# Two experts' token rows selected transposed, chunk by chunk between their products

## The chip, the cores and the metric

The kernel runs on one core of a Trainium2 chip. The metric is the device time of one execution in microseconds; the median of three runs is given with their lowest and highest. A profile of one further execution gives the rows. Times in rows are microseconds from the start of the profiled span.

## What is computed

One decoder layer on 256 tokens of 2048 channels, float32: a mixer (dilated window attention beside retention), a LayerNorm, and then a mixture of 32 experts. Each token picks one of four expert groups and in it the two best of eight experts. The part that matters here:

```python
def expert_block(args):
    xb, e = args
    hid = jax.nn.silu(xb @ w_gate[e]) * (xb @ w_up[e])
    return hid @ w_down[e]
```

w_gate[e] and w_up[e] are 2048 x 512, w_down[e] is 512 x 2048; xb are the rows of the tokens that chose expert e. The second LayerNorm follows.

## The kernel before

The first 1140 us are the mixer, the router and the first LayerNorm. Then come 32 experts, called items, each with 32 places for token rows (ROWS = 32; an expert with more tokens gets more items at the end). The weights are read from memory once each, 12.6 MB an expert, into four buffers W0 to W3 of 4 MB by DMAs that SyncE's queue issues in program order. Kind 0 is the first half of gate and up (channels in j = 0), kind 1 the second half, kind 2 the down matrix. A load waits until the products that read the buffer before have been counted: gu_used is raised by 2 after each half of gate and up, d_used after halves of the down product. Expert 1's second half comes in parts: pairs of 512 KB that wait for gu_part, which item 0's products raise behind chunks k = 1, 3 and 5 of the first half, and a last one that waits for gu_used. Expert 0's second half has its own buffers WT0. These orders are written out by hand, and the change leaves SyncE's order as it is.

For each item the token rows are made in four steps. z is the normalised layer output (tile Z, also named ZN), tokens on the partitions.
- VectorE writes a selection matrix SEL, 128 tokens x 32 places for each of the two token tiles, 1 where the token goes to that place. For item 0 and 1 this comes straight from the members and their ranks (SEL and SEL1); for later items select_next counts the places in YD down by 32 and compares again.
- `gather` on TensorE: SEL is the stationary operand, z streams through, eight products in four column groups of 32 columns each. The result has 4 x 32 rows in PSUM.
- `rows_copy` on ScalarE copies it to XG, `turn_rows` on TensorE transposes it in four blocks of 128 x 128.
- `rows_scaled` on ScalarE scales the 16 channel chunks with LayerNorm's scale and bias into XE, one instruction each. XE is the stationary operand of `gate_up`.

`gate_up(item, ..., q, ...)` multiplies chunk k of XE (32 columns) with gate and up (512 columns each). Even k use column groups 0 and 1, odd k groups 2 and 3, so four products run side by side. Item 0 sums in bank 6, item 1 in bank 0. Each product is two records in the profile. `hidden` on VectorE and `hidden_tanh` on ScalarE make the hidden values, `turn_hidden` transposes them (HB to HT), `down` multiplies with the down matrix, `spread_rows` adds the rows back to the tokens.

Around the first two items TensorE's order before is: gather(0), place_rows, turn_rows(0), count_rows, gate_up(0) first half with gather(1) behind its chunk 3 and turn_rows(1) behind chunk 5, gate_up(1) first half, gate_up(0) second half, gather(2), gate_up(1) second half, turn_hidden(0). place_rows and count_rows are three full-width products each that VectorE needs for the places of the later items.

Of the kernel before, what the change touches and what calls it, by code (L numbers as in the profile page):

```python
# [37 lines left out]
P = 128  # L38
# [3 lines left out]
KD = D // P  # L42
# [227 lines left out]
def build(nc, x, positions, w_in, w_branch_attn, w_branch_ret, w_out, ln1_scale, ln1_bias,  # L270
# [92 lines left out]
    XG0 = at("XG0", 176, [QC])  # L363
    XG1 = at("XG1", 178, [QC])
    W11 = at("W11", 44, [2 * HID])
    SEL1 = at("SEL1", 201.25, [TOK, ROWS])
# [146 lines left out]
    members, ranked, xe_first = sem("members"), sem("ranked"), sem("xe_first")  # L513
# [92 lines left out]
    def xe_bank(item):  # L606

        return SPREAD + 1 if isinstance(item, int) and item == 1 else XE_BANK

    def xg(item):  # L610

        return (XG0, XG1)[item] if isinstance(item, int) and item < 2 else XG

# [227 lines left out]
    def _(pe):  # L841
# [276 lines left out]
        def gather(item):  # L1118

            pe.wait_ge(sel_ready, item * TOK + TOK)  # L1120
            if isinstance(item, int) and item < 2:
                pe.wait_ge(z_norm, TOK)
            else:
                pe.wait_ge(xe_stored, item * QS)
            sel, bank = (SEL1 if isinstance(item, int) and item == 1 else SEL), xe_bank(item)
            for t in range(TOK):
                channels = ZN[:, t].rearrange("p (j c h k) -> p j h c k", j=QS, h=QD // QS, k=KQ * QS // QD)
                for m in range(QD):
                    mm = pe.matmul(PS[m * ROWS:(m + 1) * ROWS, bank].rearrange("p (c k) -> p c k", c=P),  # L1129
                                   sel[:, t], channels[:, m // 2, m % 2], start=t == 0, stop=t == TOK - 1)  # L1130
            mm.then_inc(gathered, 1)

        def turn_rows(item):

            pe.wait_ge(xg_stored, item + 1)
            for k in range(KD // QD):
                mm = pe.transpose(PS[:, xe_bank(item), k * P:(k + 1) * P],  # L1137
                                  xg(item)[:].rearrange("p (c k) -> p k c", c=P)[:, k], rid)
            mm.then_inc(xe_turned, 1)

        def gate_up(item, k4, q, rows, more=False, gathered_between=None, last=False):

            by_place = isinstance(item, int) and item < 2 and q == 0
# [6 lines left out]
            for m in range(2):  # L1150
# [10 lines left out]
            for j in range(KQ):  # L1161
                k = KQ * q + j
                odd = j % 2
                if by_place and j < KQ - 1:
                    pe.wait_ge(xe_first, item * (KQ - 1) + j + 1)
                elif by_place:
                    pe.wait_ge(xe_stored, item * QS + 1)
# [11 lines left out]
                if gathered_between is not None and j % 2 and j < KQ - 1:  # L1179
                    mm.then_inc(gu_part, 1)  # L1180
                    if j == 3:
                        gather(gathered_between)
                    elif j == 5:
                        turn_rows(gathered_between)
            mm.then_inc(gu_used, 2)
# [278 lines left out]
    def _(act):  # L1464
# [179 lines left out]
        def rows_copy(item):  # L1644
            act.wait_ge(gathered, item + 1)
            act.activation(xg(item)[:], PS[:, xe_bank(item)], ACT.Copy).then_inc(xg_stored, 1)

        def rows_scaled(item, buf):

            first = isinstance(item, int) and item < 2  # L1650
            act.wait_ge(xe_turned, item + 1)
            for j in range(QS):
                for k in range(KQ):
                    if first and j == 0 and k:
                        last.then_inc(xe_first, 1)
                    at_k = KQ * j + k
                    c0 = at_k % 4 * P + at_k // 4 * ROWS
                    last = act.activation(XE[:, buf, at_k], PS[:, xe_bank(item), c0:c0 + ROWS], ACT.Identity,  # L1658
# [22 lines left out]

        rows_copy(0)
        rows_scaled(0, 0)
        rows_copy(1)
        rows_scaled(1, 1)
# [777 lines left out]
```

## Time and profile before

| | |
|---|---|
| median of three runs | 2062.95 us (2062.85 to 2064.05) |
| profiled execution, its own time | 2060.22 us |
| span of its rows | 2058.1 us |
| TensorE matmul busy | 1766.7 us, 86% of the span |
| VectorE busy | 994.9 us, 48% |
| ScalarE busy | 757.1 us, 37% |
| mean DMA rate over the span | 299 GB/s |
| scaling of one chunk on ScalarE (L1658), 512 of them | median 0.41 us |
| copy to XG on ScalarE (L1646), 32 of them | median 0.60 us |
| share of DMA W<-in_w_expert_up_dram in the chain that ended last | 21% |
| share of DMA W<-in_w_expert_down_dram in it | 11% |

The span is what lies between the first and the last instruction that was profiled; the execution's own time is 2.1 us longer. Busy time of TensorE is a sum of modelled durations that overlap. The granted clock is a share of 2.4 GHz; 0.50 is 1.2 GHz.

### The profile page before, as it was taken

What the parts mean: (1) busy time and instruction counts of PE and PEld (TensorE: products, weight loads), DVE (VectorE), ACT (ScalarE), POOL (GpSimd) and SP (SyncE); (2) the same over time, 40 slices, a digit from 0 to 9 for tenths busy, and PEclk for the clock granted to TensorE, in tenths of its full rate; (3) what the DMA queues carried; (4) which work ended last, traced back from release to release, by engine and by line L of the source; (5) the groups of instructions that cost most, each with busy time, mean ns of one, the idle gap of its engine ahead of it and who ended that gap; (6) DMA issues with size and microseconds to landing.
All of it is one profiled execution on the core that took longest, in us unless ns stands there. A gap on an engine that the chain in (4) does not pass through costs nothing.

```text
span 2058.1 us, 25311 instructions
## 1 busy us (share of the span) xinstructions
PE 1766.7 (86%) x9868; PEld 1141.9 (55%) x9868; DVE 994.9 (48%) x1469; ACT 757.1 (37%) x1321; POOL 15.3 (1%) x34
## 2 busy tenths in 40 slices
PE   9999999999999999999999986666566666666667
PEld 7888888888888888888888541111112111111222
DVE  5454454555444444566565564334433433343357
ACT  5444444344444444354443422222222222222221
POOL 0000000000000000000000000000000000000000
PEclk9999999999999999999999988887888888887888
DMA  7556655455556555467677999999999999999998
GB/s 247 194 175 189 199 175 176 150 184 187 191 181 194 172 185 178 155 188 238 218 279 287 381 428 425 429 431 429 427 430 433 430 426 429 431 430 427 430 428 367
DMA packets 139042, 615.07 MB, mean 299 GB/s; under 512 B 14228, under 2 KB 14900, under 8 KB 117840
## 3 DMA queue, kind: packets, MB, share of 16 engines
q1 hardware_dynamic: 138240, 611.75, 77.5%
q0 software_dynamic: 720, 2.18, 0.6%
q8 instruction: 58, 0.95, 0.2%
q14 instruction: 24, 0.20, 0.0%
HBM read 609.61 MB, written 2.36 MB: 297 GB/s over the span
## 4 chain that ended last, share of the span: by engine, by line
PE 54%; DMA 33%; issue 10%; DVE 2%; ACT 0%; SPq 0%; DVEq 0%; POOL 0%; POOLq 0%
DMA W<-in_w_expert_up_dram 21%; PE PS L593 14%; PE PS L595 14%; PE PS L594 14%; DMA W<-in_w_expert_down_dram 11%; PE PS L1173 5%; PE PS L1224 2%; PE PS L962 1%; PE PS L1314 0%; PE PS L1129 0%; DVE ZACC L2234 0%; PE PS L1052 0%; DMA VC<-VS 0%; PE PS L1295 0%; PE PS L939 0%
## 5 line engine op out<-in xcount | busy, mean ns | idle before, releaser
L570 DVE TENSOR_TENSOR WL<-RAW,WH 128x1024 fp32r<-128x1024 f32 x384 | 457.4, 1221 | 403.9 <-ACT WH L566 402.5
L566 ACT ACTIVATE WH<-RAW 128x1024 fp32r<-128x1024 f32 x384 | 394.5, 1058 | 261.6 <-PE PS L595 199.8
L593 PE MATMUL PS<-WH,XH 128*128 128x512 f32 x1216 | 480.0, 395 | 0.1
L595 PE MATMUL PS<-WH,XL 128*128 128x512 f32 x1216 | 474.0, 390 | 0.0
L594 PE MATMUL PS<-WL,XH 128*128 128x512 f32 x1216 | 473.3, 389 | 0.0
L1173 PE MATMUL PS<-W,XE 128*32 128x512 f32 x2016 | 277.3, 698 | 135.0 <-DMA W<-in_w_expert_up_dram 133.6
L2234 DVE TENSOR_TENSOR ZACC<-PS,ZACC 128x1024 f32<-128x1024 f32 x124 | 146.0, 1219 | 294.3 <-PE PS L1295 294.3
L1224 PE MATMUL PS<-W,HT 128*32 128x512 f32 x992 | 171.0, 851 | 135.7 <-DMA W<-in_w_expert_down_dram 135.7
L593 PEld LDWEIGHTS PS<-WH,XH 128*128 128x128 f32 x1216 | 228.3, 188 | 49.3 <-issue 1.7
L595 PEld LDWEIGHTS PS<-WH,XL 128*128 128x128 f32 x1216 | 228.2, 188 | 48.3
L594 PEld LDWEIGHTS PS<-WL,XH 128*128 128x128 f32 x1216 | 228.6, 188 | 45.8
L1173 PEld LDWEIGHTS PS<-W,XE 128*32 128x32 f32 x2016 | 70.9, 125 | 322.0 <-issue 187.3
L1224 PEld LDWEIGHTS PS<-W,HT 128*32 128x32 f32 x992 | 38.5, 149 | 242.5 <-DMA W<-in_w_expert_down_dram 124.5
L1658 ACT ACTIVATE XE<-PS,LSB 128x32 f32<-128x32 f32 x512 | 141.1, 414 | 2.6 <-PE PS L1137 1.8
L1664 ACT ACTIVATE HT<-PS 128x128 f32<-128x128 f32 x32 | 9.0, 280 | 222.6 <-PE PS L1192 222.6
L2185 DVE TENSOR_TENSOR GSUM_H<-PS,GB 32x512 f32<-32x512 f32 x31 | 21.0, 679 | 140.2 <-ACT UB L1638 140.2
L1672 ACT ACTIVATE YH<-PS,WROW 128x512 fp32r<-128x512 f32 x29 | 20.0, 690 | 141.2 <-PE PS L1295 119.1
L1637 ACT ACTIVATE GB<-PS 32x512 f32<-32x512 f32 x31 | 18.3, 589 | 142.4 <-PE PS L1173 142.4
L1129 PE MATMUL PS<-Z,SEL 128*32 128x512 f32 x512 | 61.7, 598 | 0.7 <-DVE SEL L2062 0.7
L593 PE MATMUL PS<-WH,RH 128*128 128x512 f32 x128 | 50.2, 392 | 0.0
L595 PE MATMUL PS<-WH,RL 128*128 128x512 f32 x128 | 49.9, 390 | 0.0
L594 PE MATMUL PS<-WL,RH 128*128 128x512 f32 x128 | 49.8, 389 | 0.0
(333 smaller groups left out, 1472.7 us busy)
## 6 DMA issues: line engine op xcount, KB each, us to landing
RAW<-in_w_in_dram SPq DMA_DIRECT2D x304, 512.0 KB, 4.5
W<-in_w_expert_gate_dram SPq DMA_DIRECT2D x61, 2048.0 KB, 28.6
W<-in_w_expert_up_dram SPq DMA_DIRECT2D x61, 2048.0 KB, 33.0
W<-in_w_expert_down_dram SPq DMA_DIRECT2D x28, 4096.0 KB, 35.2
RAW<-in_w_branch_ret_dram SPq DMA_DIRECT2D x32, 512.0 KB, 5.2
RAW<-in_w_out_dram SPq DMA_DIRECT2D x32, 512.0 KB, 6.0
W<-in_w_expert_down_dram SPq DMA_DIRECT2D x7, 2048.0 KB, 30.4
RAW<-in_w_branch_attn_dram SPq DMA_DIRECT2D x16, 512.0 KB, 5.3
```

What stands on the lines that cost most here:

```text
L566: act.activation(WH[:, i % RING], RAW[:, i % RING], ACT.Copy).then_inc(hi_done, 1)
L570: dve.tensor_tensor(WL[:, i % RING], RAW[:, i % RING], WH[:, i % RING].bitcast(F32), ALU.subtract).then_inc(lo_done, 1)
L593: pe.matmul(PS[:, bank + t], hs, wh, start=first and j == 0, stop=False)
L594: pe.matmul(PS[:, bank + t], hs, wl, start=False, stop=False)
L595: mm = pe.matmul(PS[:, bank + t], ls, wh, start=False, stop=end)
L962: mm = pe.transpose(PS[:, bank, h * P:(h + 1) * P], NAT[:, t, h * DH:(h + 1) * DH], ident)
L1129: mm = pe.matmul(PS[m * ROWS:(m + 1) * ROWS, bank].rearrange("p (c k) -> p c k", c=P), sel[:, t], channels[:, m // 2, m % 2], start=t == 0 ...
L1173: mm = pe.matmul(PS[c0:c0 + ROWS, gu_bank(item)], rows[:, k, 0:ROWS], w[:, at_j * HID:(at_j + 1) * HID], start=k < 2, stop=k >= KD - 2)
L1224: mm = pe.matmul(PS[m * ROWS:(m + 1) * ROWS, Y_BANK], HT[:, b], W[pair_q][:, b // KB2, col:col + QC], start=b == 0, stop=b == KH - 1)
L1658: last = act.activation(XE[:, buf, at_k], PS[:, xe_bank(item), c0:c0 + ROWS], ACT.Identity, bias=LSB[:, 1, at_k:at_k + 1], scale=LSB[:, 0, ...
L2185: dve.tensor_tensor(GSUM_H[0:ROWS], PS[0:ROWS, gu_bank(item)], GB[0:ROWS], ALU.add)
L2234: dve.tensor_tensor(z, PS[:, SPREAD + 2 * n:SPREAD + 2 * n + 2], z, ALU.add).then_inc(added, 1)
```

## The change

The rows of items 0 and 1 are no longer gathered and then transposed. A chunk of 128 channels of z, which are columns at a stride of 8 floats, is now the stationary operand, 128 x 128, and the selection matrices of both items side by side (SEL01, 64 columns) stream through it. The result is the transposed chunk of both items at once: 16 such selections of two products each (one for each token tile). ScalarE scales both items' 64 columns in one instruction, 16 instead of 32. There is no rows_copy and no transpose for these items. gather, rows_copy and turn_rows stay for item 2 and later.

TensorE's order becomes a loop over k = 0 to 15: item 0's chunk k, then the selection of chunk k + 2, then, for k below 8, item 1's chunk k. Two selections and place_rows stand ahead of the loop, count_rows behind item 0's chunk 1. The results of the selections alternate between two PSUM banks. The first selection waits for both items' selection matrices. VectorE's select_next(2) overwrites SEL01 and waits for the last of the 16 selections.

```diff
@@ TensorE
+        def gather_turned(k):
+
+            bank, c0 = first_place(k)
+            a = k // KQ * KQ * P + k % KQ
+            for t in range(TOK):
+                mm = pe.matmul(PS[:, bank, c0:c0 + 2 * ROWS], ZN[:, t, a:a + KQ * P - k % KQ:KQ],
+                               SEL01[:, t].rearrange("p i r -> p (i r)"), start=t == 0, stop=t == TOK - 1)
+            mm.then_inc(first_turned, 1)
+
...
-        gather(0)
+        pe.wait_ge(sel_ready, 2 * TOK)
+        pe.wait_ge(z_norm, TOK)
+        gather_turned(0)
+        gather_turned(1)
         place_rows()
-        turn_rows(0)
-        count_rows()
-        pe.wait_ge(sel_ready, 2 * TOK)
-        gate_up(0, 0, 0, take(0), gathered_between=1)
-        gate_up(1, 1, 0, take(1))
-        gate_up(0, 0, 1, take(0))
+        for k in range(KD):
+            q, j = divmod(k, KQ)
+            gate_up(0, 0, q, take(0), places=range(j, j + 1))
+            if k == 1:
+                count_rows()
+            if k + 2 < KD:
+                gather_turned(k + 2)
+            if q == 0:
+                gate_up(1, 1, 0, take(1), places=range(j, j + 1))
         gather(2)
@@ ScalarE
-        rows_copy(0)
-        rows_scaled(0, 0)
-        rows_copy(1)
-        rows_scaled(1, 1)
+        for k in range(KD):
+            act.wait_ge(first_turned, k + 1)
+            bank, c0 = first_place(k)
+            act.activation(XE[:, :, k], PS[:, bank, c0:c0 + 2 * ROWS].rearrange("p (i r) -> p i r", i=2), ACT.Identity,
+                           bias=LSB[:, 1, k:k + 1], scale=LSB[:, 0, k:k + 1]).then_inc(
+                *((xe_first, 1) if k < KD - 1 else (xe_stored, 2 * QS)))
@@ VectorE
         def select_next(item):
 
             dve.drain()
-            dve.wait_ge(gathered, item)
+            if isinstance(item, int) and item == 2:
+                dve.wait_ge(first_turned, KD)
+            else:
+                dve.wait_ge(gathered, item - 2)
```

TensorE's instructions before, from the end of count_rows on: L1116 is its last product, L1173 is gate_up, L1129 gather(1), L1137 turn_rows(1), W_107 item 0's and W_106 item 1's weights.

```order
L1116 MATMUL PS<-AC,RC 128x32
L1173 MATMUL PS<-W_107,XE 32x512 x8
L1129 MATMUL PS<-Z,SEL_129 32x512 x8
L1173 MATMUL PS<-W_107,XE 32x512 x4
L1137 MATMUL PS<-RC,XG_127 128x128 x4
L1173 MATMUL PS<-W_107,XE 32x512 x4
L1173 MATMUL PS<-W_106,XE 32x512 x16
```

The same place now: L1128 is gather_turned with its 64 columns, L1172 gate_up, L1104 the last product of place_rows, L1108 to L1110 count_rows.

```order
L1104 MATMUL PS<-CUM,RC 128x64
L1172 MATMUL PS<-W_107,XE 32x512 x2
L1128 MATMUL PS<-SEL_127,Z 128x64 x2
L1172 MATMUL PS<-W_106,XE 32x512 x2
L1172 MATMUL PS<-W_107,XE 32x512 x2
L1108 MATMUL PS<-CUM,RC 128x32
L1109 MATMUL PS<-AC,RC 128x32
L1110 MATMUL PS<-AC,RC 128x32
L1128 MATMUL PS<-SEL_127,Z 128x64 x2
L1172 MATMUL PS<-W_106,XE 32x512 x2
L1172 MATMUL PS<-W_107,XE 32x512 x2
L1128 MATMUL PS<-SEL_127,Z 128x64 x2
```

The runs of 8, 4, 4 and 16 products in column groups have become pairs, and a full-width pair stands behind every two pairs.

VectorE's instructions at select_next(2), before, with the semaphores they wait for: YD are the places counted down, SEL the selection matrix for item 2, G and V what the router's weights are made from.

```order
L2075 TENSOR_REDUCE YPOS<-PICK 128x4
L2147 TENSOR_SCALAR YD<-YPOS 128x4
L2094 TENSOR_SCALAR YD<-YD 128x4 [waits gathered]
L2084 TENSOR_SCALAR SELF<-RC,YD 128x32 x2
L2087 SCALAR_TENSOR_TENSOR SEL<-RC,YD,SELF 128x32 x2
```

And now:

```order
L2076 TENSOR_REDUCE YPOS<-PICK 128x4
L2151 TENSOR_SCALAR YD<-YPOS 128x4
L2098 TENSOR_SCALAR YD<-YD 128x4 [waits first_turned]
L2085 TENSOR_SCALAR SELF<-RC,YD 128x32 x2
L2088 SCALAR_TENSOR_TENSOR SEL<-RC,YD,SELF 128x32 x2
```

The instructions are the same; the wait in their middle is now for the 16th selection instead of gather(1).

## Rows read from the trace of the kernel before

**Rows 1.** Busy time by stretch: stretch, length, engines, PEclk, DMA share, GB/s.
```profile
1154.00:1162.00 8.00, 8.00 (x74) 3.49 (x70) 6.32 (x39) 7.07 (x27) 0.00 (x0) 1.00 0.97 350
...
1300.00:1900.00 600.00, 384.89 (x2760) 111.76 (x2760) 238.30 (x390) 161.38 (x459) 0.00 (x0) 0.83 1.00 429
```

**Rows 2.** Chain that ended last, in order of time: start, us, what.
```profile
1224.78 21.30 DMA W<-in_w_expert_down_dram
...
1956.17 32.99 DMA W<-in_w_expert_up_dram
```

**Rows 3.** Timeline of SyncE's queue: start us, us, issue of a DMA.
```profile
1154.16 0.35 SPq L764 DMA_DIRECT2D W<-in_w_expert_gate_dram  x1
...
1163.09 0.43 SPq L655 DMA_DIRECT2D W<-in_w_expert_up_dram  x1
1171.31 0.33 SPq L673 DMA_DIRECT2D W<-in_w_expert_down_dram  x1
1177.85 0.33 SPq L655 DMA_DIRECT2D W<-in_w_expert_gate_dram  x1
...
1192.77 0.38 SPq L655 DMA_DIRECT2D W<-in_w_expert_up_dram  x1
1218.37 0.33 SPq L655 DMA_DIRECT2D W<-in_w_expert_gate_dram  x1
```

**Rows 4.** DMA issues at 1154.16, 1163.09, 1171.31, 1192.77: KB, us to landing.
```profile
W<-in_w_expert_gate_dram SPq DMA_DIRECT2D x1, 512.0 KB, 4.4
...
W<-in_w_expert_up_dram SPq DMA_DIRECT2D x1, 2048.0 KB, 13.6
...
W<-in_w_expert_down_dram SPq DMA_DIRECT2D x1, 4096.0 KB, 15.6
...
W<-in_w_expert_up_dram SPq DMA_DIRECT2D x1, 2048.0 KB, 33.4
```

**Rows 5.** Timeline of VectorE and TensorE, 1148 to 1172 us: start, us, instruction.
```profile
1148.80 0.42 DVE L2066 SCALAR_TENSOR_TENSOR SEL<-RC,PS,AC 128x32 f32<-128x32 f32 x2
1148.94 1.92 PE L1129 MATMUL PS<-Z,SEL 128*32 128x512 f32 x16 [0.70 <-DVE SEL L2062]
...
1150.80 0.43 PE L1108 MATMUL PS<-AC,RC 128*128 128x64 f32 x2
...
1151.26 0.41 PE L1110 MATMUL PS<-CUM,RC 128*128 128x64 f32 x2
...
1152.53 0.39 PE L1116 MATMUL PS<-AC,RC 128*128 128x32 f32 x2
...
1152.89 2.09 PE L1173 MATMUL PS<-W,XE 128*32 128x512 f32 x16
...
1165.91 1.90 PE L1129 MATMUL PS<-Z,SEL 128*32 128x512 f32 x16
1167.63 3.62 PE L1173 MATMUL PS<-W,XE 128*32 128x512 f32 x32
1171.18 0.66 PE L1192 MATMUL PS<-RC,HB 32*128 32x32 f32 x4
```

**Rows 6.** Timeline of VectorE at select_next(2) and hidden(0).
```profile
1159.24 0.17 DVE L2094 TENSOR_SCALAR YD<-YD 128x4 f32<-128x4 f32 x1
...
1159.95 0.41 DVE L2087 SCALAR_TENSOR_TENSOR SEL<-RC,YD,SELF 128x32 f32<-128x32 f32 x2
...
1167.38 0.68 DVE L2185 TENSOR_TENSOR GSUM_H<-PS,GB 32x512 f32<-32x512 f32 x1 [3.08 <-ACT UB L1638]
```

**Rows 7.** Weight loads by line, ns min/median/max: L1137 stride 4, L1052 contiguous.
```profile
L1137 PEld LDWEIGHTS PS<-RC,XG x128: 195/212/220, 1151.6 to 2003.0; 128*128 128x128 f32 x128
...
L1052 PEld LDWEIGHTS PS<-WR,ZT x16: 192/192/203, 1141.5 to 1143.2; 128*128 128x128 f32 x16
```

**Rows 8.** A stretch at the lower clock, and gate_up in it.
```profile
1210.00:1215.00 5.00, 4.23 (x24) 1.30 (x28) 3.51 (x5) 0.00 (x0) 0.00 (x0) 0.50 0.99 419
...
1211.93 6.20 PE L1173 MATMUL PS<-W,XE 128*32 128x512 f32 x32
```

More of the change, by code:

```diff
@@ L604, in gu_bank, with first_place @@
         return 6 if isinstance(item, int) and item == 0 else GU_BANK
[L606 to L612, printed above, removed]
+    def first_place(k):
+        return (XE_BANK, SPREAD + 1)[k % 2], k // 2 * 2 * ROWS
     def norm_bank(j):
@@ L1120, in gather @@
             pe.wait_ge(sel_ready, item * TOK + TOK)
[L1121 to L1125, printed above, removed]
+            pe.wait_ge(xe_stored, item * QS)
             for t in range(TOK):
@@ L1128, in gather, with gate_up @@
                 for m in range(QD):
-                    mm = pe.matmul(PS[m * ROWS:(m + 1) * ROWS, bank].rearrange("p (c k) -> p c k", c=P),
-                                   sel[:, t], channels[:, m // 2, m % 2], start=t == 0, stop=t == TOK - 1)
+                    mm = pe.matmul(PS[m * ROWS:(m + 1) * ROWS, XE_BANK].rearrange("p (c k) -> p c k", c=P),
+                                   SEL[:, t], channels[:, m // 2, m % 2], start=t == 0, stop=t == TOK - 1)
             mm.then_inc(gathered, 1)
+        def gather_turned(k):
[5 more added lines that the diff above has]
+            mm.then_inc(first_turned, 1)
         def turn_rows(item):
-            pe.wait_ge(xg_stored, item + 1)
+            pe.wait_ge(xg_stored, item - 1)
             for k in range(KD // QD):
-                mm = pe.transpose(PS[:, xe_bank(item), k * P:(k + 1) * P],
-                                  xg(item)[:].rearrange("p (c k) -> p k c", c=P)[:, k], rid)
+                mm = pe.transpose(PS[:, XE_BANK, k * P:(k + 1) * P],
+                                  XG[:].rearrange("p (c k) -> p k c", c=P)[:, k], rid)
             mm.then_inc(xe_turned, 1)
-        def gate_up(item, k4, q, rows, more=False, gathered_between=None, last=False):
-            by_place = isinstance(item, int) and item < 2 and q == 0
+        def gate_up(item, k4, q, rows, more=False, last=False, places=range(KQ)):
+            by_place = isinstance(item, int) and item < 2
             if not by_place:
@@ L1149, in gate_up @@
                 pe.wait_ge(part_landed, 16 * 6)
-            for m in range(2):
+            for m in range(2) if places[0] == 0 else ():
                 if apart:
@@ L1160, in gate_up @@
                     pe.wait_ge(w_landed[pair_q][1], item * 8 + (16 * loads_until(q, k4, (0, 1)) - 8 * k4))
-            for j in range(KQ):
+            for j in places:
                 k = KQ * q + j
                 odd = j % 2
-                if by_place and j < KQ - 1:
-                    pe.wait_ge(xe_first, item * (KQ - 1) + j + 1)
+                if by_place and k < KD - 1:
+                    pe.wait_ge(xe_first, k + 1)
                 elif by_place:
-                    pe.wait_ge(xe_stored, item * QS + 1)
+                    pe.wait_ge(xe_stored, 2 * QS)
                 for m in range(2):
@@ L1178, in gate_up @@
                         pe.wait_ge(late_landed[m], 16)
-                if gathered_between is not None and j % 2 and j < KQ - 1:
+                if isinstance(item, int) and item == 0 and q == 0 and odd and j < KQ - 1:
                     mm.then_inc(gu_part, 1)
[L1181 to L1185, printed above, removed]
+            if places[-1] == KQ - 1:
+                mm.then_inc(gu_used, 2)
         def turn_hidden(item):
@@ L2061, in _ @@
         for t in range(TOK):
[L2062 removed]
+            dve.scalar_tensor_tensor(SEL01[:, t, 0], RC[:, R_IOTA:R_IOTA + ROWS], PS[:, 6, 2 * t:2 * t + 1],
                                      AC[:, t, 0:1].broadcast_to((P, ROWS)), ALU.is_equal,
```

20 lines of the change are left out of this document (7 added, 13 removed).

## The prediction

> **What bounds the kernel now.** I read the stretches first, then the chain that ended last, then the DMA issues with their landings, and last the timeline of the stretch that the change touches. In [rows 1] the reader is to see a DMA share of 1.00 at 429 GB/s from 1300 to 1900 us, and 350 GB/s in the 8 us from 1154 to 1162, at nearly the same share. The chain in order of time is made of loads of expert weights from 1224 us on [rows 2]: TensorE waits for them and not they for it, down to 1989 us. So from here on the time of the end is the time at which the stream of weights gets through its fixed bytes, and the question is not what the first two experts cost on TensorE, but whether the queue of loads runs dry sooner or later than now. All gains are bounded by what the stream loses now between 1154 and 1162 us: 8 x (429 - 350) / 429 = 1.5 us.
>
> **How a load lands.** From the issues [rows 3] and their times to landing [rows 4] a rule can be read off. The 512 KB load issued at 1154.16 landed after 4.4 us; its bytes at 429 GB/s are 1.2 us, so 3.2 us are delay. A load thus lands at the later of (landing of the one before, its issue + 3.2), plus its bytes at 429 GB/s (2048 KB 4.9 us, 4096 KB 9.8 us). Test: the up half issued at 1163.09 landed at 1176.7; the whole down matrix issued at 1171.31 should land at 1176.7 + 9.8 = 1186.5, and landed at 1171.31 + 15.6 = 1186.9. Its slack was 1176.7 - 3.2 - 1171.31 = 2.2 us: an issue later by more than that leaves the queue empty, and nothing gives that back. The next thin place is the load issued at 1218.37: the one before it (1192.77 + 33.4) landed at 1226.2, so its slack was 4.6 us. The loads between have more: at 1177.85 it is 1186.9 - 3.2 - 1177.85 = 5.9, and it grows from there to 1192.77, whose load took 33.4 us to land.
>
> **What is removed.** On TensorE two gathers and two sets of four transposes; on ScalarE two copies of 0.6 us (table above) and 16 of 32 scalings. ScalarE's part of that is worth nothing: the rows of TensorE follow each other from 1152.89 on without an idle time in front that names ScalarE [rows 5]. TensorE's part is 2 x 1.7 us for the gathers and the transposes beside them, and it comes back below as full-width products.
>
> **What is added: the order on TensorE.** Instead of runs of 16 products in four column groups, each channel chunk k is now: two products of expert 0 in two column groups, two full-width selections (128x128 stationary, 64 columns), two products of expert 1 in the same two groups; from k = 8 expert 0 alone. Expert 1's products for k and expert 0's for k + 1 use opposite groups and stand next to each other, so they run together. Price of one round, from [rows 5]:
> - A product of 512 columns is two records in one column group. gather(2)'s 16 records run from 1165.91 to the start of the next line at 1167.63, 1.72 us for four steps of four records, 0.43 us a step. With two or four groups at work a round needs two steps, 0.86 us; behind k = 8 half the array stands idle in it.
> - From column groups to full width: the last of the gather's four steps starts at 1148.94 + 3 x 0.43 = 1150.23, and the first full-width product at 1150.80, 0.57 after it, so 0.14 us beyond the step.
> - Full-width products: L1108 at 1150.80 and L1110 at 1151.26 are two apart, 0.23 us each.
> - Back to groups: L1116 starts at 1152.53, gate_up at 1152.89: 0.36 us.
>
> The sum is 0.86 + 0.14 + 0.23 + 0.36 = 1.59, say 1.6 us. The same four products without a selection between them, four groups at work, take two steps or 0.86 us. The Trainium skill's page TensorEngine Tiling (Key Properties) says that a change of tiling mode drains the engine; the 0.14 us is this trace's size of that, and the larger loss is that the drain separates products that filled four groups together.
>
> **The start.** The first selection now waits for both experts' columns: 1148.80 + 0.42 = 1149.2 instead of the first two, so it starts at 1149.3. Four full-width products and the three of place_rows: 6 x 0.23 + 0.36 = 1.7; round 0 starts at 1151.1. The scalings do not hold it: each round asks ScalarE for one row, which it now does in 0.41 us (table above) for half the columns, and the selection runs two chunks ahead.
>
> **Sum to the next gather.** Fourteen rounds (k = 0 to 13) have a selection, plus count_rows 0.7: 1151.1 + 14 x 1.6 + 0.7 = 1174.2 for k = 14, and 15 runs beside it; TensorE is free at 1175.1. VectorE's select_next(2) waits for the last selection, since it overwrites the shared tile: that starts in round 13 at 1173.6 and is done about 1174.2. YD to SEL takes 1159.24 to 1160.36, 1.1 us [rows 6], so gather(2) starts at about 1175.6 against 1165.91: 9.7 us later. From there to the end of expert 1's second half are 1171.18 - 1165.91 = 5.3 us, to 1180.9.
>
> **A second wait behind it.** VectorE's list behind SEL (weights, diagonals, counts) runs from 1160.36 to 1167.38 - 3.08 = 1164.30, 3.9 us; it was covered by 3.08 us of idleness before hidden(0). Now it ends at 1179.4, while hidden(0) could have begun at about 1176.5. From hidden(0)'s first row at 1167.38 to turn_hidden(0) at 1171.18 are 3.8 us, so that stands at 1183.2, 12.0 us later. Everything behind it on TensorE (the row sums, the down product, gate_up of expert 2) moves with it.
>
> **What the stream of weights makes of it.**
> - The small parts follow k = 1, 3, 5, 7 of expert 0: 1153.8 (now 1154.16), then 1157.6, 1160.8 and 1163.9; the halves for expert 2 follow at 1165.5 and 1165.9 instead of up to 1163.09. By the rule the queue is dry for 0.7 to 0.9 us ahead of each of the three later ones, and the up half for expert 2 lands at 1178.5 instead of 1176.7.
> - The down matrix of expert 1 waits for expert 1's second half: issued at 1181.0 instead of 1171.31, it lands at 1181.0 + 3.2 + 9.8 = 1194.0 instead of 1186.9: **7.1 us lost**.
> - The next ones come 12.0 us later and find the queue full (1177.85 + 12.0 + 3.2 = 1193.1, against 1194.0).
> - The thin place: 1218.37 + 12.0 + 3.2 = 1233.6 against 1226.2 + 7.1 = 1233.3: 0.3 us more.
>
> Together 7.4 us. The sum is made on the profiled execution: 2060.22 + 7.4 = 2067.6; the median of the runs is 2.7 us above that execution, so 2070.3.
>
> **The stationary operand's stride** is the unknown. The new loads read z at a stride of 8 floats, and no load here does. The nearest rows [rows 7]: stride 4 takes 212 ns, contiguous 192 ns, and in [rows 5] two records with a contiguous load fit into 0.23 us. I take that, since 20 ns a load more are lost in the rounding to 1.6; less than contiguous is not possible. The upper bound is twice, 0.23 a record, so with four records 0.5 us a round. On this the Trainium skill's page SBUF — State Buffer (section Door 1: The DMA port swizzle) says that memory lines are 16 bytes and that four floats are as far as one strides for free. It puts no number on the penalty. By the row, the sum is 2070.3; with the doubled load it is the third case below.
>
> **The cases.** The measurement tells 0.2%, 4.1 us, from no change.
> 1. As worked out, round between 1.45 and 1.75 us: 2070.3, own range 2068 to 2073. **0.60.**
> 2. Not slower: the switches are hidden. For it speaks that weight loads do run ahead in the gathers; against it both switches in the rows. Then a round is 0.86 + 2 x 0.23 = 1.3 us, 0.3 x 14 = 4.2 us less: the down matrix is issued at 1176.8, 3.0 us are lost, 2066. The point that decides is a round of 1.37 us. **0.17.**
> 3. The stride doubles the loads: 14 x 0.5 = 7 us more, all of it into the down matrix's issue: 2077. **0.10.**
> 4. The clock falls. In [rows 8] the granted clock is 0.50 (1.2 GHz of 2.4) and gate_up takes 6.20 us, against 3.62 in [rows 5]; before it the engine had done light products and stood idle. For it speaks half an array idle from k = 8; against it that gate_up ran at full speed behind the light products of 1150.8 to 1152.9. At 1.7 times, the rounds cost 16 us more: 2086. **0.08.**
> 5. Nothing of the delay reaches the stream (overlap of rounds that I do not see), and the small gap of 1.5 us closes: 2061.5. **0.05**, and with run to run noise 0.02 of it below -0.2%.
>
> Slower 0.78, same 0.20, faster 0.02. The range goes from case 2 to case 3, 2065 to 2078, and leaves out case 4 and most of case 5.
>
> **What would show it.** Right: rounds of 1.6 us, with a gap of about 0.1 us on each change to full width; gather(2) near 1175.6; VectorE waiting some 15 us ahead of YD; the first down load issued near 1181 and a hole in the DMA share of some 4 to 5 us around 1179 to 1184; the same 429 GB/s after it, and a last stretch unchanged but for 7 us. Wrong: a round of 1.3 us or less; a weight load of 0.4 us for z; a granted clock of 0.5 between 1150 and 1175 us; or a hole near 1230 us, where I count 0.3 us and a slower chain of normalisation rows would make it some us.

## The result, and the profile after

The changed kernel takes 2083.2 us (median of four runs, 2078.2 to 2084.3) against 2062.9 us before (four runs, 2061.1 to 2064.1). The ratio is 1.0096, with a 95% interval of 1.0083 to 1.0108: 20.3 us slower. The direction was as forecast; the size lies outside the range of 2065 to 2078. The profiled execution is the slowest, 2084.31 us. In the experiments below three executions (one of the kernel before beside e1 to e4, e10's profiled one and one of e14) took 1.8 to 2.8 times as long as the others and are left out of all medians.

The stretches of the changed kernel, as in [rows 1] (stretch, length, PE, PEld, DVE, ACT, POOL, PEclk, DMA share, GB/s):

```profile
1150.00:1152.00 2.00, 2.00 (x12) 2.00 (x12) 0.00 (x0) 0.61 (x2) 0.00 (x0) 1.00 1.00 426
1152.00:1155.00 3.00, 3.00 (x11) 1.22 (x10) 0.00 (x0) 0.20 (x1) 0.00 (x0) 0.51 0.93 386
...
1160.00:1165.00 5.00, 5.00 (x21) 1.56 (x18) 3.85 (x25) 0.77 (x2) 0.00 (x0) 0.50 0.32 129
1165.00:1170.00 5.00, 5.00 (x24) 2.17 (x24) 0.16 (x1) 0.81 (x2) 0.00 (x0) 0.50 0.60 210
1170.00:1175.00 5.00, 5.00 (x28) 2.41 (x24) 0.00 (x0) 0.81 (x2) 0.00 (x0) 0.75 0.59 206
...
1190.00:1195.00 5.00, 5.00 (x50) 2.60 (x48) 4.39 (x22) 1.18 (x2) 0.00 (x0) 1.00 0.00 0
...
1300.00:1900.00 600.00, 392.51 (x2788) 113.13 (x2779) 235.03 (x384) 156.64 (x441) 0.00 (x0) 0.83 1.01 429
```

Two things are to be seen. The DMA share falls to a third and, from 1190 to 1195 us, to nothing, and from 1300 us on it is full at the same 429 GB/s: the loss is the queue that ran dry, as the prediction's theory has it. And the granted clock is 0.50 from 1152 to about 1172 us, where TensorE is busy without a pause.

TensorE's timeline of the changed kernel, answering to [rows 5]:

```profile
1149.64 2.12 PE L1128 MATMUL PS<-SEL,Z 128*128 128x64 f32 x8 [1.03 <-DVE SEL L2067]
...
1168.87 1.94 PE L1172 MATMUL PS<-W,XE 128*32 128x512 f32 x8
1170.74 1.21 PE L1128 MATMUL PS<-SEL,Z 128*128 128x64 f32 x4
1171.88 1.37 PE L1172 MATMUL PS<-W,XE 128*32 128x512 f32 x8
...
1178.45 1.05 PE L1172 MATMUL PS<-WT,XE 128*32 128x512 f32 x4
1179.43 1.16 PE L1128 MATMUL PS<-SEL,Z 128*128 128x64 f32 x4
1180.52 1.05 PE L1172 MATMUL PS<-WT,XE 128*32 128x512 f32 x4
...
1190.11 2.11 PE L1119 MATMUL PS<-Z,SEL 128*32 128x512 f32 x16
1197.48 0.66 PE L1188 MATMUL PS<-RC,HB 32*128 32x32 f32 x4 [1.82 <-DVE HB L2195]
```

At full clock a round takes 1180.52 - 1178.45 = 2.07 us, at half clock 1171.88 - 1168.87 = 3.01 us; forecast was 1.6. gather(2) starts at 1190.11 (forecast 1175.6, before 1165.91), turn_hidden(0) at 1197.48 (forecast 1183.2). The eight records of the first two selections take 1.95 us from their start to L1102 at 1151.59, 0.24 us each, and this at full clock: their loads, by line (ns min/median/max, first and last start):

```profile
L1128 PEld LDWEIGHTS PS<-SEL,Z x64: 312/334/337, 1149.6 to 1188.4; 128*128 128x128 f32 x64
```

The up half for expert 2 and the down matrix of expert 1, answering to [rows 3, 4], in SyncE's queue:

```profile
1177.82 0.43 SPq L649 DMA_DIRECT2D W<-in_w_expert_up_dram  x1
1195.69 0.33 SPq L667 DMA_DIRECT2D W<-in_w_expert_down_dram  x1
```

with their KB and us to landing:

```profile
W<-in_w_expert_up_dram SPq DMA_DIRECT2D x1, 2048.0 KB, 13.0
...
W<-in_w_expert_down_dram SPq DMA_DIRECT2D x1, 4096.0 KB, 13.8
```

The up half landed at 1190.8, the down matrix at 1209.5, 22.6 us after the 1186.9 of before. The rule gives 1195.69 + 3.2 + 9.8 = 1208.7. The landing of the thin place moved by 23.1 us (its load, issued at 1243.20, took 11.0 us), so nearly the whole loss stood at the down matrix, and none at the thin place: the load ahead of it landed 23.1 us later too. The profiled executions differ by 2084.3 - 2060.2 = 24.1 us.

### The profile page after: what moved, and what is told of

The parts are those of the page before. It is cut to its first block, busy times and chain, and to the rows that moved or that the text cites. A ratio compares the mean times of both kernels' runs of the same rounds, so it can differ in the third digit from the quotient of the medians.

```text
span 2082.2 us, 25302 instructions
## 1 busy us (share of the span) xinstructions
PE 1787.5 (86%) x9892; PEld 1155.3 (55%) x9892; DVE 995.0 (48%) x1469; ACT 754.4 (36%) x1303; POOL 15.3 (1%) x34
## 4 chain that ended last, share of the span: by engine, by line
PE 54%; DMA 33%; issue 10%; DVE 2%; SPq 0%; DVEq 0%; ACT 0%; POOL 0%; POOLq 0%; ACTq 0%
DMA W<-in_w_expert_up_dram 20%; PE PS L591 14%; PE PS L593 14%; PE PS L592 14%; DMA W<-in_w_expert_down_dram 12%; PE PS L1172 5%; PE PS L1220 2%; PE PS L1128 1%; PE PS L956 1%; PE PS L1310 0%; DVE ZACC L2238 0%; DMA VC<-VS 0%; PE PS L1046 0%; PE PS L1291 0%; PE PS L933 0%
## 5 line engine op out<-in xcount | busy, mean ns | idle before, releaser
L1172 PE MATMUL PS<-W,XE 128*32 128x512 f32 x2016 | 283.8, 707 | 137.5 <-DMA W<-in_w_expert_up_dram 136.0
L1172 PEld LDWEIGHTS PS<-W,XE 128*32 128x32 f32 x2016 | 70.6, 125 | 320.6 <-issue 184.1
L1657 ACT ACTIVATE XE<-PS,LSB 128x32 f32<-128x32 f32 x480 | 132.8, 416 | 0.8
```

The costliest lines, as they stand in the source:

```text
L1172: mm = pe.matmul(PS[c0:c0 + ROWS, gu_bank(item)], rows[:, k, 0:ROWS], w[:, at_j * HID:(at_j + 1) * HID], start=k < 2, stop=k >= KD - 2)
L1657: last = act.activation(XE[:, buf, at_k], PS[:, XE_BANK, c0:c0 + ROWS], ACT.Identity, bias=LSB[:, 1, at_k:at_k + 1], scale=LSB[:, 0, at_k: ...
```

## The experiments

Differences are to the median of before in the same call (2062.5 us for e1 to e4, 2062.4 for e5 to e8, 2064.0 for e9 to e12, 2063.2 for e13 to e16, 2061.8 for e17), so times of different calls compare only to some 2 us. Ratios and their 95% intervals are estimated from all executions and can differ a little from the ratio of the medians.

**1. Where TensorE's time goes: the stride, the idle time, both.** Three kernels in one call. The first fills the idle time ahead of the first selection; the second takes contiguous columns of z, so that it selects other channels and its sums are of other channels, with the same work; the third does both.

```diff
+        keep_busy(2, 2, rid, RC[:, R_IOTA:R_IOTA + CH])     # behind the ranked product
...
-            a = k // KQ * KQ * P + k % KQ
+            a = k * P
-                mm = pe.matmul(PS[:, bank, c0:c0 + 2 * ROWS], ZN[:, t, a:a + KQ * P - k % KQ:KQ],
+                mm = pe.matmul(PS[:, bank, c0:c0 + 2 * ROWS], ZN[:, t, a:a + P],
```

> The changed kernel with two idle-filling products (128 x 512, 1.7 us at full clock) between the rank products and the first selection. Theory (two causes side by side: z's strided weight loads make a round 2.08 us, and the granted clock at 0.50 from 1152 to 1172 us makes seven rounds 3.0 us): if the fill holds the clock, all rounds take 2.08 us, the next gather starts some 6 us earlier than 1190.1, the down load with it, and the time is about 2077. Rival (the clock's fall is caused by the light products of the rounds themselves, not by the idle time ahead of them): the clock falls all the same, some us later, and the time stays within 3 us of 2083.

> The changed kernel with 128 neighbouring columns of z as the stationary operand instead of every eighth; the channels then do not match the weights' rows, so the sums are of other channels, with the same number of instructions and bytes. Theory A (the stride is what doubles a weight record's distance from 0.115 to 0.237 us, and the slow light loads also let the clock fall): records at 0.115, round 1.6 us, clock 1.00, time 2069 to 2071. Theory B (the stride costs 0.5 us a round, the clock falls for another reason, the idle TensorE ahead of the first selection): records at 0.115, but 0.50 clock again over several rounds, time about 2075. Rival C (the stride costs nothing, the record's distance comes from the change of mode): records stay at 0.237 and the time at 2083.

> Both edits: neighbouring columns of z (sums of other channels) and the two filling products. This takes both extra causes away, so what is left is the order of the products alone, a round of 1.6 us by the sum of the prediction: time 2070 to 2072 with 0.8 us for the fill. If the order costs nothing by itself, 2063.

Measured: e1 2079.4 us (ratio 1.0080 [1.0063, 1.0097]), e2 2071.1 (1.0042 [1.0028, 1.0056]), e3 2072.2 (1.0046 [1.0029, 1.0063]). e3 against e1 is 7.2 us for the stride alone. e1's first theory came about in the clock, and less in the time: its down matrix was issued at 1191.25 us, 4.4 us earlier than in the changed kernel. Of e2's theories A came about; e3 took what was expected. The contiguous kernel is the one that the prediction had worked out. Its timeline, loads and queue:

```profile
1167.09 0.66 PE L1128 MATMUL PS<-SEL,Z 128*128 128x64 f32 x4
1167.67 1.05 PE L1172 MATMUL PS<-WT,XE 128*32 128x512 f32 x4
1168.66 0.66 PE L1128 MATMUL PS<-SEL,Z 128*128 128x64 f32 x4
...
1182.61 0.66 PE L1188 MATMUL PS<-RC,HB 32*128 32x32 f32 x4 [1.82 <-DVE HB L2195]
```

```profile
L1128 PEld LDWEIGHTS PS<-SEL,Z x64: 186/192/192, 1149.5 to 1173.7; 128*128 128x128 f32 x64
```

```profile
1180.83 0.33 SPq L667 DMA_DIRECT2D W<-in_w_expert_down_dram  x1
```

A round is 1168.66 - 1167.09 = 1.57 us (forecast 1.6), turn_hidden(0) stands at 1182.6 (1183.2), the down matrix is issued at 1180.8 (1181.0), and it landed 13.7 us later at 1194.5 (1194.0). The profiled execution is 2071.1 - 2060.2 = 10.9 us longer than before, though, and the down matrix landed only 7.6 us later. Part of the rest stands at the pair of loads behind it:

```profile
1180.00:1185.00 5.00, 3.18 (x15) 1.32 (x8) 2.74 (x8) 2.29 (x5) 0.00 (x0) 0.83 0.70 236
1185.00:1190.00 5.00, 5.00 (x35) 1.94 (x37) 3.86 (x6) 3.53 (x12) 0.00 (x0) 0.82 1.04 447
```

```profile
1190.96 0.33 SPq L649 DMA_DIRECT2D W<-in_w_expert_gate_dram  x1
```

Behind the rounds the clock fell for a few us, and the pair (1190.96 and 1191.33) was issued 13.1 us later than before, where the prediction had 12.0. Its slack was 1194.5 - 3.2 - 1190.96 = 0.3 us, and it landed at 1200.3 and 1206.9, against 1199.4 and 1204.3 by the rule. Four down matrices on, 1.6 us of this are still there (a landing at 1314.1 against 1304.9, 9.2 us later). e3, e16 and e14 show the same, 1.7 to 2.0 us with the clock fallen in the same place; the changed kernel's first profile, e1, e5 and e15, with 1.00 there, show 0.3 us or less, and e9, with a fall, 0.4. On the change of mode, the Trainium skill's page TensorEngine Tiling (Key Properties) has that it drains the engine; these rounds agree: 1.57 us against the 0.86 us of the same four products in a run is what the changes of mode, the selection between them and the half-filled groups cost together.

**2. Where the time counts: the slack of the down load.** The kernel before with products added behind gather(2), 6.0 us (e4) and 1.7 us (e8) of TensorE:

```diff
         gather(2)
+        keep_busy(Y_BANK, 7, rid, RC[:, R_IOTA:R_IOTA + CH])    # e8: 2 instead of 7
```

> The kernel before with seven filling products (6.0 us) behind gather(2), ahead of the second half of expert 1. Theory (a delay of TensorE costs only what empties the queue of loads): the down load is issued at 1177.3 instead of 1171.3, lands 3.8 us later than 1186.9, and the time is 3.8 us longer, 2066.7. Rival (TensorE's delay passes to the end in full): 6.0 us, 2068.9. Rival (loads are hidden anyway): no change.

> The kernel before with two products of 512 columns more (1.7 us of TensorE) behind the gather of expert 2: the first down load is issued some 1.7 us later, at 1173.0. Theory of the slack (2.2 us; e4_before_delay7 with 6.0 us cost 4): no change, 2062.6 to 2063.2. Rival (the time follows TensorE's path directly): 1.7 us more, 2064.3.

e4: 2066.9 us, 1.0019 [1.0010, 1.0029], 4.4 us for 6.0. e8: 2062.2 us, 0.9997 [0.9989, 1.0006], nothing for 1.7. So delay becomes time only beyond some 2 us: 6.0 - 2.2 = 3.8 was the theory's figure. The rival that a delay passes on in full is left out by e8, whose interval ends at 1.2 us; e4's alone, 2.1 to 6.0 us, would hardly do it.

**3. Which stride is dear.** The selections at strides of 4, 2 and 3 floats, other channels each time, same work:

```diff
-            a = k // KQ * KQ * P + k % KQ
+            a = k // 4 * 4 * P + k % 4          # e9: 2 for 4, e16: 3 for 4, its chunk 15 from column 0
-                mm = pe.matmul(PS[:, bank, c0:c0 + 2 * ROWS], ZN[:, t, a:a + KQ * P - k % KQ:KQ],
+                mm = pe.matmul(PS[:, bank, c0:c0 + 2 * ROWS], ZN[:, t, a:a + 4 * P - k % 4:4],
```

> As the changed kernel, but the stationary operand of the selections takes z's columns at a stride of 4 floats (16 bytes) instead of 8 (32 bytes); it selects other channels, so the sums are of other rows, and the amount of work is the same. The contiguous version ran 2071.1 us with records 0.115 us apart, stride 8 ran 2083.2 us with records 0.237 us apart. Theory A, a line of 16 bytes: up to stride 4 a load costs about the same as a contiguous one (the selections of the experts behind use stride 4 and their rows showed 212 against 192 ns): records 0.12 us apart, clock 1.00 throughout, 2071 to 2072 us. Theory B, the load slows in proportion to the stride: records near 0.175 us apart, a round of 1.83 us, 14 x 0.23 = 3.2 us later, 2075 us.

> The changed kernel with the selections' stationary operand at a stride of 2 floats (8 bytes); other channels are selected, same amount of work. Stride 4 and stride 8 both stood 0.237 us apart, contiguous 0.115. Theory A (any stride doubles the load): loads of about 325 ns in the records, 0.237 us apart, a full-clock round of 2.08 us, and 2078 us at full clock, with the chance of executions some 5 to 8 us longer in which the clock falls. Theory B (the price grows with the stride up to 4 floats): 0.15 to 0.18 us apart, 2073 to 2075 us.

> The changed kernel with the selections' stationary operand at a stride of 3 floats (12 bytes); other channels, same amount of work. Stride 2 cost nothing measurable (210 ns a load, 2070.9 us), stride 4 and 8 the full price (325 and 331 ns, 0.237 us apart). If the price depends on how many 16-byte pieces a load touches, 3 floats lie between: 250 to 290 ns a load, 0.17 to 0.20 us apart, 2073 to 2076 us. If it is a step at 4 floats: 210 ns, 2071. If a step above 2: as stride 4, 2078 at full clock.

Their loads by line (in e16 the line is 1129), first e9 with stride 2, then e16 with 3, then e5 with 4:

```profile
L1128 PEld LDWEIGHTS PS<-SEL,Z x64: 194/196/331, 1149.6 to 1175.8; 128*128 128x128 f32 x64
```

```profile
L1129 PEld LDWEIGHTS PS<-SEL,Z x64: 250/261/264, 1150.7 to 1178.9; 128*128 128x128 f32 x64
```

```profile
L1128 PEld LDWEIGHTS PS<-SEL,Z x64: 308/329/332, 1150.1 to 1182.0; 128*128 128x128 f32 x64
```

| stride, floats | load, median ns | round at full clock, us | time, us | ratio |
|---|---|---|---|---|
| 1 (e2) | 192 | 1.57 | 2071.1 | 1.0042 [1.0028, 1.0056] |
| 2 (e9) | 196 | 1.61 | 2070.9 | 1.0037 [1.0022, 1.0051] |
| 3 (e16) | 261 | 1.84 | 2075.1 | 1.0058 [1.0044, 1.0073] |
| 4 (e5) | 329 | 2.07 | 2082.6 | 1.0104 [1.0084, 1.0123] |
| 8 (changed kernel) | 334 | 2.07 | 2083.2 | 1.0096 [1.0083, 1.0108] |

Both theories of e5 fell, the cheap one and the one in proportion: stride 4 pays in full. Both theories of e9 fell too, stride 2 costs next to nothing, and for stride 3 the first of three answers came. The price fits how many of the wanted floats share 16 bytes: with two or more to a line it is at most 4 ns a load, with one it is 137 to 142 ns, and at a stride of 3 floats, where four of them lie on three lines, it is half of that. A price that rises evenly from 2 to 4 floats would give the same 261 ns; no run here tells the two apart. At the lower clock the price is not seen: four loads of e9 at stride 2 between 1153 and 1154 us, at 0.50, took up to 331 ns, and those of the changed kernel at stride 8 and 0.50 had a median of 335. The Trainium skill's page SBUF — State Buffer (Door 1: The DMA port swizzle) gives a line of 16 bytes, at least two hits a line for full speed, and four floats as the stride that is still free. The loads agree with the first two statements; against the last, e5's 329 ns decides.

**4. Why the nearest row had misled.** In [rows 7] a stationary operand at a stride of 4 floats loads in 212 ns. Those are transposes. e17 is the kernel before with them written as products of the same operands:

```diff
-                mm = pe.transpose(PS[:, xe_bank(item), k * P:(k + 1) * P],
-                                  xg(item)[:].rearrange("p (c k) -> p k c", c=P)[:, k], rid)
+                mm = pe.matmul(PS[:, xe_bank(item), k * P:(k + 1) * P],
+                                  xg(item)[:].rearrange("p (c k) -> p k c", c=P)[:, k], rid, start=True, stop=True)
```

> The kernel before, with the transposes of the gathered rows (stationary operand at a stride of 4 floats, 212 ns a load) written as products of the same operands with the identity. Theory (a transpose's load is spared the price that a product's load pays): loads of 325 ns and two records a product, as the two products of the end that take a stationary operand at that stride (304 to 315 ns), against 192 for contiguous ones. Rival (it is the tile, not the kind of operation): loads stay at 212 ns. In time: the transposes of the first two experts take about twice as long (0.75 us more each), which lies within the slack of 2.2 us: 2062.5 to 2064.

The loads of e17:

```profile
L1137 PEld LDWEIGHTS PS<-RC,XG x256: 307/329/332, 1152.3 to 2007.3; 128*128 128x128 f32 x128
```

212 ns have become 329, with two records a product for one a transpose. A set of four takes 2.13 us in e17's timeline, and 0.75 before:

```profile
1152.34 2.13 PE L1137 MATMUL PS<-RC,XG 128*128 128x128 f32 x8
```

```profile
1151.58 0.75 PE L1137 MATMUL PS<-RC,XG 128*128 128x128 f32 x4
```

That is 1.4 us more a set, where I had counted 0.75, and it stands ahead of the small parts of the weights too: the first was issued at 1156.31 us against 1154.16 (0.76 us of that stood in this execution ahead of the set already), and the up half landed at 1179.7 against 1176.7. Measured: 2064.8 us, 1.0012 [1.0002, 1.0021], 3.0 us more by the medians and 2.5 by the ratio, where the expectation had 2062.5 to 2064. The trace of before held a row of the right kind, the products of the end that take ROW1 at a stride of 4 floats (L1342), beside the same with contiguous columns (L1328):

```profile
L1342 PEld LDWEIGHTS PS<-LN2H,ROW x2: 303/304/304, 2026.5 to 2034.7; 4*128 4x128 f32 x2
```

```profile
L1328 PEld LDWEIGHTS PS<-LN2H,ROW x8: 181/182/183, 2027.5 to 2042.4; 4*128 4x128 f32 x8
```

**5. The order apart from the method.** Selections in four runs of four chunks, each run in its own bank and ScalarE waiting for a run's end (these two edits are left out below), at stride 8 (e6) and contiguous (e7):

```diff
-        gather_turned(0)
-        gather_turned(1)
+        for k in range(8):
+            gather_turned(k)
         place_rows()
-        for k in range(KD):
...
+        for g in range(4):
+            q, j = divmod(4 * g, KQ)
+            gate_up(0, 0, q, take(0), places=range(j, j + 4))
+            if g == 0:
+                count_rows()
+            if q == 0:
+                gate_up(1, 1, 0, take(1), places=range(j, j + 4))
+                for k in range(4 * g + 8, 4 * g + 12):
+                    gather_turned(k)
```

> The changed kernel's selections, at their stride of 8 floats, in four runs of four chunks (8 full-width products) instead of one chunk at a time, each run in a bank of its own; ScalarE waits for a run's end. The expert products then go 16 at a time with all four column groups at work. Three changes back to column groups remain instead of fifteen. Theory (half-filled groups and changes of mode are the price of the order): selections at 0.237 us a product: 1149.65 + 3.8 + 0.7 = 1154.2 for the first expert product, then 12 places of 1.8 us less, in sum 1154.2 + 6 x 1.8 + 0.7 + 2 x 2.4 = 1170.5 for the next gather (1190.1 in the changed kernel, 1165.9 before), the first down load 5.3 us later at 1175.8, landing 1188.9 against 1186.9, so 2065 us at full clock. If the clock falls again as in the changed kernel (sixteen slow loads in a row at the start), up to 8 us of TensorE time more: 2070 to 2073. Rival (the turned selection itself is dear, not its order): above 2078.

> As e6_batched, but with contiguous columns of z as the stationary operand (other channels are selected, same amount of work). Theory: selections at 0.115 us: the next gather at 1166.5, the first down load near 1171.8, within its slack of 2.2 us, clock 1.00: 2063 us, as before the change. It then shows that the 8 us of e2_contiguous over before are the alternation alone. Rival: the wait for both experts' columns and the later parts of the weights cost some us whatever the order: 2066 or more.

e7: 2065.9 us, 1.0021 [1.0012, 1.0029]. e6: 2078.7 us, 1.0071 [1.0058, 1.0084]. e7 against e2 is 5.2 us: the price of alternating, with what it brings on at the loads behind the down matrix. The rest of e2's 8.6 us, some 3.5 us, stays with a better order too, as e7's rival had it. Part of the reason is in e7's rows:

```profile
1149.91 3.79 PE L1128 MATMUL PS<-SEL,Z 128*128 128x64 f32 x32 [1.03 <-DVE SEL L2067]
1153.53 0.39 PE L1102 MATMUL PS<-AC,RC 128*128 128x64 f32 x2
...
1158.79 2.00 PE L1128 MATMUL PS<-SEL,Z 128*128 128x64 f32 x16
1160.72 3.64 PE L1172 MATMUL PS<-W,XE 128*32 128x512 f32 x32
```

A chunk is four records (two token tiles, two records a product), so 16 chunks are 1153.53 - 1149.91 + 2 x 1.93 = 7.5 us even when contiguous. Two gathers and two sets of transposes were 2 x 1.72 + 2 x 0.75 = 4.9 us. My expectations for e6 and e7 had counted half of the records; e7's forecast was 2063. The down matrix was issued at 1175.1, 3.8 us later than before, but that is not the wait that ends last: the up half ahead of it landed only at 1180.2 (1176.7 before), and from there the rule gives 1180.2 + 9.8 = 1190.0 for the down matrix, which landed at 1189.9, 3.0 us late. The up half was late because the third pair of small parts was issued at 1161.85 instead of 1157.59: in this order item 1's first 8 products and a run of selections stand ahead of item 0's chunk 5. So e7's loss is at the small parts. In e6 the first run alone took 7.67 us (32 records), and the clock fell in it. e6 is 16 us slower than before, where 2065 was expected at full clock and 2070 to 2073 with a fall; its rival, that the strided selection is dear in any order, comes nearest.

**6. The clock.** e1 had kept 1.00 from 1150 to 1175 us, where the changed kernel shows 0.50 up to 1172:

```profile
1152.00:1155.00 3.00, 3.00 (x17) 2.55 (x17) 0.00 (x0) 0.81 (x2) 0.00 (x0) 1.00 0.96 403
1155.00:1160.00 5.00, 5.00 (x34) 3.03 (x30) 1.27 (x5) 0.81 (x2) 0.00 (x0) 1.00 0.36 111
```

Ahead of this, e1's profile has a short fall of its own:

```profile
1145.00:1150.00 5.00, 5.00 (x11) 2.05 (x9) 3.25 (x23) 3.24 (x4) 0.00 (x0) 0.74 1.00 415
```

So does e8's, the kernel before with other products added (0.89 and 0.77 from 1140 to 1150 us). By e1's profile alone the fall could have been moved and not prevented; e15's shows 1.00 from 1140 to 1215 us and is the clean one.

Six runs asked what brings the fall: e10 and e13, one kernel in two calls, are e6 with e1's filling products; e11 has only the first two chunks contiguous, e12 only those strided (other channels in the contiguous ones); e14 and e15 are the changed kernel and e1 again, side by side.

```diff
-            a = k // KQ * KQ * P + k % KQ
+            a, step = (k * P, 1) if k < 2 else (k // KQ * KQ * P + k % KQ, KQ)    # e12: k >= 2
-                mm = pe.matmul(PS[:, bank, c0:c0 + 2 * ROWS], ZN[:, t, a:a + KQ * P - k % KQ:KQ],
+                mm = pe.matmul(PS[:, bank, c0:c0 + 2 * ROWS], ZN[:, t, a:a + step * P - (k % KQ if step > 1 else 0):step],
```

> e6_batched (the right channels, selections in runs of four chunks) with two filling products of 512 columns behind the ranked counts, in TensorE's idle time ahead of the first selection (they start the selection about 1 us later). The four executions of e6_batched at a mean granted clock of 0.922 to 0.926 took 2076.8 to 2079.2 us, the one at 0.929 took 2073.5. Theory (idle time and slow loads together let the clock fall, and the fall is the rest of the loss): the clock stays at 1.00 between 1150 and 1175 us in most executions, 2074 to 2075 us. Rival (a long run of slow loads alone lets it fall): 2077 to 2080.

> The changed kernel with only the first two chunks' selections contiguous (other channels in those two), the other fourteen at a stride of 8 floats. Theory 1 (the clock falls for what follows the idle time at once: 1 us idle, then eight slow records): clock 1.00 in all executions, 0.5 us less TensorE time at the start, 2077 to 2078. Theory 2 (slow loads among the rounds let it fall wherever they stand): falls in some executions as in the changed kernel, median 2080 or more.

> The counterpart: the first two chunks' selections at a stride of 8 floats, the other fourteen contiguous (other channels in those). Theory 1 (idle time with the slow records right behind it): the clock falls to 0.50 in some executions around 1152 to 1165 us, those take 2075 or more, the others 2071.5. Theory 2 (slow loads in the rounds): clock 1.00, 2071 to 2072 in all, as e2_contiguous plus 0.5.

> e10_batched_fill once more, for its profile: its executions took 2075.8 to 2079.8 us at a mean granted clock of 0.923 to 0.928. If the long run of 32 slow records lets the clock fall although TensorE was kept busy ahead of it, the profile shows 0.50 from within the run at about 1153 to 1156 us, and 2076 to 2080 us; if it shows 1.00 up to 1175 us, the time is to be 2074.5 and the loss lies elsewhere.

> The changed kernel itself once more, beside e15: executions of two kinds, near 2078 us with the clock at 1.00 from 1150 to 1175 us, and 2083 to 2088 us with 0.50 there; both kinds are to appear, the slower in half of them or more (3 of 4 so far).

> e1_fill once more beside e14. If filling the idle time lowers the chance of the fall: nearly all executions between 2077 and 2080 us. If e1's four executions were luck: the same two kinds as e14 plus 1 us, median 2083 or more.

Medians: e10 2078.4 us (1.0071 [1.0058, 1.0084]), e11 2078.5 (1.0071 [1.0058, 1.0084]), e12 2074.5 (1.0058 [1.0040, 1.0077]), e13 2078.0 (1.0067 [1.0053, 1.0082]), e14 2081.7 (1.0094 [1.0078, 1.0111]), e15 2078.4 (1.0076 [1.0063, 1.0089]). e10's theory (2074 to 2075) fell: with filling products this order took what e6 had taken, and e13 gives its profile. The single executions tell more:

| kernel | executions, us |
|---|---|
| changed kernel, nine | 2078.0, 2078.2, 2078.5, 2081.7, 2083.1, 2083.2, 2084.3, 2086.3, 2086.7 |
| with filling products (e1, e15), nine | 2077.4 to 2080.1 |
| stride 4 (e5), four | 2077.7, 2078.4, 2086.7, 2088.5 |
| first chunks contiguous (e11), five | 2077.1, 2077.3, 2078.5, 2078.6, 2083.4 |
| first chunks strided (e12), six | 2071.9, 2072.4, 2072.7, 2076.2, 2079.9, 2083.0 |
| contiguous (e2), five | 2070.0 to 2073.1 |

So the changed kernel has one time near 2078 and, in two of three executions, 3 to 9 us more. In the profiles the extra goes with a fall of the clock; for executions without a profile only the mean clock is known (0.930 and 0.931 for the three near 2078, 0.924 to 0.928 for the six others). Where e11 was profiled in its longest execution, 0.50 stands from 1152 to 1170 us, although its first loads were contiguous: theory 1 of e11 is not all of it, and theory 2's median of 2080 or more was not reached either, with one long execution in five. e12's profile, one of its three longer executions, has 0.50 from 1152 to 1171 us and bears its theory 1 out. Nine executions with the filling products and nine without (five of each side by side, e15 and e14) show that idle time is a part: none above 2080.1 against six. But the fall comes without idle time too, as in e13, where TensorE was busy ahead of the selections and the clock fell within the run of 32 slow records, which it began at 1150.12:

```profile
1150.00:1152.00 2.00, 2.00 (x10) 1.88 (x9) 0.00 (x0) 0.00 (x0) 0.00 (x0) 1.00 1.00 426
1152.00:1155.00 3.00, 3.00 (x15) 3.00 (x14) 0.00 (x0) 1.01 (x4) 0.00 (x0) 0.77 0.93 388
1155.00:1160.00 5.00, 5.00 (x26) 4.23 (x29) 0.00 (x0) 1.57 (x5) 0.00 (x0) 0.50 0.08 30
```

And a fall can stand elsewhere. e14's profiled execution, 2081.7 us, has 1.00 from 1150 to 1190 us and then, as TensorE waits for the hidden values:

```profile
1190.00:1195.00 5.00, 3.79 (x8) 1.96 (x9) 3.09 (x9) 1.95 (x4) 0.00 (x0) 0.66 1.00 369
```

Its down matrix was issued at 1189.43, 6.3 us earlier than in the changed kernel's first profile; that is the fall's price at the place that counts. From the rows it is 20 x (1 - 2.07 / 3.01) = 6.2 us. The end is only 2.6 us earlier: e14's own fall delays the pair of loads behind the down matrix as in e2, and 1.7 us of that are still there four down matrices on.

## Why the prediction was wrong

Its own steps, in order:
- **Stream of weights, landing rule, slack: right.** 429 GB/s after 1300 us as before, a DMA share of 0.00 while the down matrix was awaited, e8 and e4 on either side of 2.2 us, and, in the changed kernel's profiled execution, a time (24.1 us more) near the shift of its down matrix (22.6).
- **Price of a round without the stride, start, wait of VectorE behind the last selection, second wait behind it: right.** e2 gave 1.57 us for 1.6, 1180.8 for 1181.0, and turn_hidden(0) waited 1.82 us for HB. To the sum's 7.4 us belong e2's 7.6 us at the down matrix; the 0.3 us at the thin place were not seen.
- **"The next ones come 12.0 us later and find the queue full": too tight to say, and wrong in e2.** The prediction left them 0.9 us (1193.1 against 1194.0), and counted TensorE at full clock up to there. In e2 they came 13.1 us later with the clock fallen and cost some 1.6 us. That e2's 2071.1 lies so near the forecast 2070.3 is in part luck: the forecast had added 2.7 us for the median over the profiled execution, while e2's profiled execution is its median.
- **The stationary operand's stride: this step failed, and it made the sum too small.** "I take that, since 20 ns a load more are lost in the rounding" rested on the transposes of [rows 7]; a product's load at that stride takes 329 ns, not 212, and a record 0.24 us, not 0.115. It was the third case, given 0.10, whose 7 us have the right size: 2078.2 - 2071.1 = 7.1 us between the executions at full clock.
- **The clock: the second step that failed.** The fourth case had it, given 0.08, for another reason (the half-idle array from k = 8) and with 16 us. It falls before that, from 1152 us, and costs about 6 us at the down matrix. What sets it off stays open. In e2's profile, with the same half-filled groups, the clock holds at 1.00 through all the rounds, so half an array idle did not bring it there.
- **The cases as rivals: failed with them.** Cases 3 and 4 stood side by side, one chance each, though six of nine executions at stride 8 ran long and none of e2's five did. They came together: order 8.6, stride 7.1, clock 5.0 (2083.2 - 2078.2), in sum 20.7 us. As these are steps from one median to the next, their sum is the measured 20.3 by construction and no test of them. With the two joined the range would have reached past 2083.
- Case 2 (switches hidden, a round of 1.3 us) and case 5 fell with e2's rounds.

## What to carry to other kernels

Before an operand is read in a new pattern, look in the trace for a row of the same kind of instruction in the same pattern: a transpose is no measure of a product's load, and the right row may stand in quite another part of the kernel. Where a stream of transfers sets the end, find the one issue whose slack the change uses up; a delay costs nothing up to the slack and all of itself beyond. Two unlikely cases of which one brings on the other get a joint chance.

## What the runs showed of the hardware

- A product's load of a 128 x 128 float32 stationary operand took 192 ns with contiguous columns, 196 at a stride of 2 floats, 261 at 3, 329 at 4 and 334 at 8; a transpose's took 212 at 4. At a granted clock of 0.50 strides 2 and 8 took the same (331 and 335).
- Short pairs of products in column groups with a full-width pair of contiguous loads between them run in rounds of 1.57 us, where the same four without it took two steps, 0.86 us.
- The granted clock fell to 0.50 while TensorE showed no pause in its rows, in some executions of a kernel and not in others, for about 20 us in the changed kernel, e11 and e12, for 3 us in e9 (stride 2). What decides between them is not settled: idle time ahead of the slow loads makes it likelier, neither it nor strided loads right behind it are needed (e13, e11), and slow loads may not be either: of 12 executions of e7, with contiguous loads, two took 2070 us and more at a lower mean clock (0.925 against 0.928 to 0.932). Other places for the filling products were not tried.
